# Second block's input tiles reordered, its norms and rotations moved between them, hidden chunks interleaved, one semaphore split

## What is computed

```python
x = first_block(...)      # dilated attention + pooling, gates, then 16384 experts of which 8 x 16 are used per token
# second block
h, hc = modulate(rmsnorm(x)), modulate(rmsnorm(ctx))            # 256 own and 256 context tokens
p = h @ w_in                                                    # 2048 -> q 1024, k 1024, v 1024, c_q 384, c_kv 256, k_rope 64
c_q, c_kv = rmsnorm(c_q) * q_norm_w, rmsnorm(c_kv) * kv_norm_w
q_mla, kv = c_q @ w_uq, c_kv @ w_ukv                            # 8 heads: 128 plain and 64 rotated columns of q, 128 k, 128 v
q_da, k_da, q_rope, k_rope = rope(...)                          # own tokens only
o = concat(diff_attention(q_da, k_da, v_da), attention(q_mla, k_mla, v_mla))
x = x + g1 * (o @ w_o)
g, u = split(modulate(rmsnorm(x)) @ w_up)                       # 2048 -> 2 x 5632
x = x + g2 * ((silu(conv3(g)) * u) @ w_down)                    # 5632 -> 2048
return rmsnorm(x)
```

## Time and profile before

| | |
|---|---|
| median of 3 runs | 3757.69 us (3756.13 to 3762.12) |
| the profiled execution: its own time | 3757.86 us |
| its span, first to last instruction | 3756.1 us |
| mean granted TensorE clock | 0.98 |
| input tiles of the second block, last matmul | 2684.0 us into the span |
| attention's first scores | 2773.4 us |
| stage "down", first matmul | 3481.3 us |

### The profile page before, as it was taken

How to read it: one execution, slowest core, us unless ns; L and a number is a source line. 1 busy time by engine, 2 the same in 40 slices (tenths; PEclk the granted TensorE clock), 3 DMA queues, 4 the chain that set the end, 5 groups by cost and what they waited for, 6 DMA issues and landing times.

```text
span 3756.1 us, 71853 instructions
## 1 busy us (share of the span) xinstructions
PE 3535.3 (94%) x27438; PEld 3378.2 (90%) x27438; DVE 2528.3 (67%) x4250; ACT 1734.2 (46%) x3141; POOL 116.6 (3%) x209
## 2 busy tenths in 40 slices
PE   1799999989999999999999999999988999999998
PEld 0799888988999999999999999889746899999998
DVE  7886432888757787878787888632266576766554
ACT  0542211454955454545454445632245565555443
POOL 0000000000200000000000000000000000000000
PEclk8899999999999999999999999999999999999999
DMA  9886775753666768676777777432210455555554
GB/s 411 340 331 254 280 275 221 265 181 135 222 250 225 300 239 314 238 300 249 285 265 288 263 289 269 171 105 97 82 53 23 157 191 191 196 194 183 175 179 146
DMA packets 118189, 829.33 MB, mean 221 GB/s; under 512 B 13105, under 2 KB 13233, under 8 KB 26801
## 3 DMA queue, kind: packets, MB, share of 16 engines
q1 hardware_dynamic: 88416, 619.20, 45.3%
q0 software_dynamic: 29520, 206.58, 14.4%
HBM read 806.86 MB, written 16.78 MB: 219 GB/s over the span
## 4 chain that ended last, share of the span: by engine, by line
PE 86%; DVE 5%; DMA 5%; ACT 3%; issue 1%; SPq 0%; POOL 0%; DVEq 0%; ACTq 0%
PE ps L1053 23%; PE ps L1054 23%; PE ps L1055 22%; PE ps L1028 9%; DMA arena<-in_ada 2%; ACT arena L549 2%; PE ps L1115 1%; PE ps L1117 1%; PE ps L1118 1%; DMA ring<-in_peer_down 1%; PE ps L1086 1%; DMA gates_scratch<-arena 1%; PE ps L1405 1%; PE ps L1042 0%; DVE ring_low L1552 0%
## 5 line engine op out<-in xcount | busy, mean ns | idle before, releaser
L549 ACT ACTIVATE w_parts<-ring 128x512 fp32r<-128x512 f32 x1288 | 801.3, 634 | 970.6 <-PE ps L1055 736.7
L1055 PE MATMUL ps<-x_high,ring_low 128*128 128x256 f32 (+1 forms) x4192 | 1182.8, 282 | 0.0
L1552 DVE TENSOR_TENSOR ring_low<-ring,w_parts 128x512 fp32r<-128x512 f32 x1288 | 836.6, 689 | 443.2 <-ACT w_parts L549 406.3
L1053 PE MATMUL ps<-x_high,w_parts 128*128 128x256 f32 (+1 forms) x2784 | 795.3, 286 | 82.2 <-DVE ring_low L1552 63.7
L1055 PEld LDWEIGHTS ps<-x_high,ring_low 128*128 128x128 f32 x4192 | 791.5, 189 | 7.8
L1054 PE MATMUL ps<-x_low,w_parts 128*128 128x256 f32 (+1 forms) x2784 | 792.9, 285 | 0.0
L1053 PEld LDWEIGHTS ps<-x_high,w_parts 128*128 128x128 f32 x2784 | 526.8, 189 | 91.8 <-DVE ring_low L1552 64.1
L1054 PEld LDWEIGHTS ps<-x_low,w_parts 128*128 128x128 f32 x2784 | 526.9, 189 | 8.2
L1552 DVE TENSOR_TENSOR ring_low<-ring,w_parts_ff 128x512 fp32r<-128x512 f32 (+1 forms) x544 | 357.7, 675 | 223.2 <-ACT w_parts_ff L549 217.3
L1053 PE MATMUL ps<-at_high,w_parts 128*128 128x256 f32 x1792 | 497.2, 277 | 0.0
L1055 PE MATMUL ps<-at_high,ring_low 128*128 128x256 f32 x1792 | 494.8, 276 | 0.0
(11 more groups left out here) (251 smaller groups left out, 5832.0 us busy)
## 6 DMA issues: line engine op xcount, KB each, us to landing
ada<-in_ada POOLq DMA_DIRECT2D x160, 1024.0 KB, 6.9
ring<-in_peer_down SPq DMA_DIRECT2D x128, 1024.0 KB, 4.9
ring<-in_peer_up SPq DMA_DIRECT2D x128, 1024.0 KB, 5.2
ring<-in_w_in SPq DMA_DIRECT2D x102, 1024.0 KB, 5.5
ring<-in_w_up SPq DMA_DIRECT2D x88, 1024.0 KB, 4.8
ring<-in_w_down SPq DMA_DIRECT2D x64, 704.0 KB, 4.0
arena<-in_ada SPq DMA_DIRECT2D x32, 1024.0 KB, 19.4
ring<-in_w_out SPq DMA_DIRECT2D x16, 1024.0 KB, 4.8
```

Of the source, the lines that this page charges most:

```text
L549: return nc.scalar.activation(*a, **k)
L1053: mm(to, w_high, high(k), start=(k == 0), stop=False)
L1055: ins = mm(to, w_low, high(k), start=False, stop=(k == k_all - 1))
L1552: vv.tensor_tensor(ring_low[:, slot, cols], ring[:, slot, cols], parts[:, m, 0:w].bitcast(F32), ALU.subtract).then_inc(lo_ready, 1)
```

## The change

- The order in the tables, in `w_in_2` and in every stream becomes q2, c2, k2, v2, then uq, then ukv. All loops over k2 and v2 on TensorE are written out. The columns of `w_uq` are put with the rotated part first.
- The norms of c_kv and c_q: ACT squares after k2's first output copy; TensorE sums after k2's third tile, c_q's into bank 5 (`b=5`); ACT takes the roots at tiles 18 and 19 of its loop, DVE the rest at 19 and 20. The squares and the rotations' temporaries lie in the free part of `cb`.
- The rotations of q2 and k2 (0 to 7): TensorE does two after each pair of v2 tiles; DVE does them at tiles 25, 27 and 29 of its loop and after the loop. Those of k_rope and the rotated part of q (8 to 12) lie between uq's tiles on TensorE.
- `hidden_high` and `hidden_low` become one buffer [44, 2, 256] at 32 KB: each chunk's low part directly behind its high part. `w_parts_ff` moves to 120 KB + 64 bytes.
- `G0`'s transfers count on a semaphore of their own, `g0_in`. DVE's `gate_held` waits for that alone; ACT waits for both.

```diff
-                  ("ahead", 16), ("first", 16), ("peer", 224), ("q2", 8), ("k2", 8), ("v2", 8), ("c2", 6), ("ukv", 16), ("uq", 16),
+                  ("ahead", 16), ("first", 16), ("peer", 224), ("q2", 8), ("c2", 6), ("k2", 8), ("v2", 8), ("uq", 16), ("ukv", 16),
...
-        HH, HL = split_room("hidden_high", 32, FF, T), split_room("hidden_low", 92 + 2 * APART, FF, T)
-        WF = split_room("w_parts_ff", 76 + APART, DEEP, PB * P)
+        hidden_both = split_room("hidden", 32, FF, 2, T)
+        HH, HL = hidden_both[:, :, 0, :], hidden_both[:, :, 1, :]
+        WF = split_room("w_parts_ff", 120 + APART, DEEP, PB * P)
...
                 pool_e.dma_start(G0[n // 8][:, n % 8, :], stage[n % 2][:, 0:16, :].rearrange("p c t -> p (c t)"))\
-                    .then_inc(g_stored[n % 2], 16)
+                    .then_inc(g0_in[n % 2], 16)
...
-                        act.wait_ge(g_stored[j], 32 * i)
+                        act.wait_ge(g0_in[j], 16 * i)
+                        act.wait_ge(g_stored[j], 16 * i)
...
                 if half:
                     for j in range(2):
-                        dve.wait_ge(g_stored[j], 32 * NBLK // 2)
+                        dve.wait_ge(g0_in[j], 16 * NBLK // 2)
...
@@ SP @@
+            for t in range(4):
+                load(TILES["uq"] + t, A["w_uq_2"][t], first + 30 + t, 12 * P)
             for t in range(2):
-                load(TILES["ukv"] + t, A["w_ukv_2"][t], first + 30 + t)
-            for t in range(4):
-                load(TILES["uq"] + t, A["w_uq_2"][t], OUTS["ukv"] if t < 2 else OUTS["ukv"] + 8 * (t - 1), 12 * P)
+                load(TILES["ukv"] + t, A["w_ukv_2"][t], OUTS["uq"] + 4 * (t + 1))
...
@@ ACT @@
+                if n == 18:
+                    root_of("kv", TA)
+                if n == 19:
+                    root_of("q", T)
...
+                if n == 15:
+                    act.wait_ge(acc_free, BANKS + OUTS["c2"] + 6)
+                    act_fn(sq_kv, ckv, ACT.Square).then_inc(squared, 1)
+                    act_fn(sq_q, cq, ACT.Square).then_inc(squared, 1)
-            act.wait_ge(acc_free, BANKS + OUTS["ukv"])
-            norm("kv", ckv, kn[:, 0:2, :], None, cols=TA)
-            norm("q", cq, sq2[:, 0:3, :], None)
...
@@ TensorE @@
+            for n in range(8):
+                o = OUTS["k2"] + n
+                bank(o)
+                split_tile("k2", 0, 0, n, ps[:, o % BANKS, :], W2, lambda k: X2H[:, k, :], lambda k: X2L[:, k, :],
+                           (14 + n) % RING)
+                if n == 2:
+                    norm_sum("kv", sq_kv, 2, TA)
+                    norm_sum("q", sq_q, 3, b=5)
+            def turn_rope(n):
+                if n >= 2:
+                    pe.wait_ge(roped, 12 + n - 1)
+                src, w = rope_step(n)
+                mm(ps[:, 4 + n % 2, 0:w], cst("perm2"), src, start=True, stop=True).then_inc(rotated, 1)
+            for m in range(4):
+                bank(OUTS["v2"] + 2 * m + 1)
+                split_values("v2", 0, 0, m,
+                             lambda tb: ps[:, (OUTS["v2"] + 2 * m + tb // 2) % BANKS, (tb % 2) * T:(tb % 2 + 1) * T],
+                             W2, X2H, X2L, 4, turn=22)
+                if m == 0:
+                    pe.wait_ge(acc_free, BANKS + OUTS["v2"])
+                    pe.wait_ge(var_ready, NORM_AT["q"] + 1)
+                turn_rope(2 * m)
+                turn_rope(2 * m + 1)
+            pe.wait_ge(scaled, before("q", "scaled") + 3)
+            for t in range(4):
...
+                if t == 1:
+                    turn_rope(8)
+                if t > 1:
+                    pe.wait_ge(acc_free, BANKS + OUTS["uq"] + 8)
+                    turn_rope(2 * t + 5)
+                    turn_rope(2 * t + 6)
             for t in range(2):
...
-            for n in range(13):
-                if n >= 2:
-                    pe.wait_ge(roped, 12 + n - 1)
...
@@ DVE @@
+                if n == 19:
+                    dve.wait_ge(final_ready, KC)
+                    norm("kv", ckv, ckv, vc("kv_norm_w_2"), cols=TA)
+                if n == 20:
+                    norm("q", cq, cq, vc("q_norm_w_2"), b=5)
+                if n in (25, 27, 29):
+                    turn_rope(n - 25)
+                    turn_rope(n - 24)
+            turn_rope(6)
+            turn_rope(7)
...
+            for n in range(8, 13):
+                turn_rope(n)
             dve.wait_ge(lam_exp, 1)
...
             dve.wait_ge(acc_free, BANKS + OUTS["wo2"])
-            for n in range(13):
-                src, w = rope_step(n)
```

More of the change, by code:

```diff
@@ L63 @@
 for _name, _n in (("qk", 24), ("v", 12), ("gate", 36), ("branch", 8), ("wo", 16), ("wq", 16),
-                  ("ahead", 16), ("first", 16), ("peer", 224), ("in2", 30), ("ukv", 2), ("uq", 4), ("wo2", 16), ("up", 88), ("down", 64)):
+                  ("ahead", 16), ("first", 16), ("peer", 224), ("in2", 30), ("uq", 4), ("ukv", 2), ("wo2", 16), ("up", 88), ("down", 64)):
     TILES[_name] = _t
@@ L396, in build_program @@
         g_stored = [sem(f"g_stored{j}") for j in range(2)]
+        g0_in = [sem(f"g0_in{j}") for j in range(2)]
         held_gated = sem("held_gated")
@@ L855, in out_copy, with root_of @@
                 return act_fn(to, src, ACT.Copy)
+            def root_of(name, cols):
+                act.wait_ge(var_ready, NORM_AT[name] + 1)
+                act_fn(rs[:, 0:cols], rs[:, 0:cols], ACT.Sqrt).then_inc(std_ready, 1)
             for n in range(31):
@@ L1016, in bank, with norm_sum @@
                 pe.wait_ge(acc_free, o + 1)
[L1018 removed]
+            def norm_sum(name, sqd, n, cols=T, b=4):
                 for k in range(n):
@@ L1056, in piece, with split_tile @@
                 return ins
-            def split_tile(name, i, per, u, to, parts, high, low):
+            def split_tile(name, i, per, u, to, parts, high, low, slot=None):
                 for j in range(PIECES):
@@ L1099, in split_summed, with split_values @@
                     sum_squares(run, c, c + 1, sq1, last=(c == KC - 1))
-            def split_values(name, i, per, m, bank_of, parts, high, low, tbs):
+            def split_values(name, i, per, m, bank_of, parts, high, low, tbs, turn=0):
                 for t in range(2):
@@ L1339, in _ @@
                 split_tile("c2", 0, 0, n, ps[:, o % BANKS, 0:TA - lo], W2, lambda k: X2H[:, k, lo:],
-                           lambda k: X2L[:, k, lo:])
-            norm_sum("kv", kn[:, 0:2, :], 2, TA)
-            pe.wait_ge(var_ready, NORM_AT["kv"] + 1)
-            norm_sum("q", sq2, 3)
-            pe.wait_ge(scaled, before("q", "scaled"))
+                           lambda k: X2L[:, k, lo:], n % RING)
+            for n in range(8):
[23 more added lines that the diff above has]
+            for t in range(4):
+                tile = TILES["uq"] + t
+                pe.wait_ge(w_slot[tile % RING], 16 * (tile // RING + 1))
+                for n in range(4):
+                    o = OUTS["uq"] + 4 * t + n
+                    bank(o)
+                    blocks(ps[:, o % BANKS, 0:T], tile, 3, lambda k: cq[:, k, :], at=3 * n).then_inc(acc_full, 1)
+                if t == 1:
[4 more added lines that the diff above has]
+                    turn_rope(2 * t + 6)
             for t in range(2):
@@ L1356, in _ @@
                     ins.then_inc(acc_full, 1)
-            pe.wait_ge(scaled, before("q", "scaled") + 3)
-            for t in range(4):
-                tile = TILES["uq"] + t
-                pe.wait_ge(w_slot[tile % RING], 16 * (tile // RING + 1))
-                for n in range(4):
-                    o = OUTS["uq"] + 4 * t + n
-                    bank(o)
-                    blocks(ps[:, o % BANKS, 0:T], tile, 3, lambda k: cq[:, k, :], at=3 * n).then_inc(acc_full, 1)
-            pe.wait_ge(acc_free, BANKS + OUTS["wo2"])
-            for n in range(13):
-                if n >= 2:
-                    pe.wait_ge(roped, 12 + n - 1)
-                src, w = rope_step(n)
-                mm(ps[:, 4 + n % 2, 0:w], cst("perm2"), src, start=True, stop=True).then_inc(rotated, 1)
+            pe.wait_ge(acc_free, BANKS + OUTS["wo2"])
             def s2(u):
```

71 lines of the change are left out of this document (32 added, 39 removed).

## The result

The changed kernel takes 3716.42 us (median of 4 runs, 3715.32 to 3722.56), the kernel before 3756.91 beside it (4 runs, 3753.40 to 3762.12): a ratio of 0.989, 95% interval 0.9879 to 0.9902. The prediction was 3713.3 us, range 3709.5 to 3731. The profiled executions took 3716.17 and 3757.86 us, with spans of 3714.4 and 3756.1: 41.7 us apart, where 44.5 were forecast.

What follows compares the result with a forecast made beforehand. TensorE, busy 94% of the span, was taken as the bound, so only its waits and matmul pace could gain: 26.4 + 2.3 + 15.8 = 44.5 us off 3757.86 gives 3713.3 us, range 3709.5 to 3731.

Steps and rivals of the forecast that it cites:

- Part 1: Second block's inputs to attention: moved norms and rotations leave TensorE no waits, 65.1 us for 91.5, 26.4 us gained.
- 8.17 us inside the input tiles: TensorE's matmuls for both norms' sums and rotations 0 to 5, still paid among the input tiles.
- 54.38 behind them: After the input tiles: rotations 6 to 12, uq and ukv's two tiles on TensorE without waits, 54.38 us.
- 2.52 for lambda: Tail before attention: ACT's last copy, table and exponential, and two tiny DVE operations, 2.52 us.
- Part 2: End of the gates: DVE starts earlier by waiting only for the 128 KB; 2.3 us gained, range 0 to 3.1.
- Part 3: Stage "down": hidden chunks side by side bring matmuls from 120.8 to 113.3 ns, 15.8 us gained.
- 885 matmuls in a window: Sign in "down": 885 matmuls in 100 us if right; 830 if wrong, putting the time near 3729.
- The rival that the layout does nothing: In "down", pieces or the sums' length cause the 120.8 ns; time 3729.1 us, chance 0.19.
- the worse layout: In "down", moving reads back and forth within 2 KB cost more; 3769.6 us at 140 ns per matmul, chance 0.03.
- both slow stages are those whose moving reads jump by an odd distance: Step for "down" and v2: odd distances between moving operands mark slow stages; "down" at 120.8 ns, v2 at 117.8.
- the weights' 64 bytes: In "down", weights stay offset by 64 bytes as in "up", so "up"'s 113.3 ns was taken.
- The start of attention gained no clock: Attention's first scores and next step: 0 us counted for a fuller clock, 1.4 us kept for the range.

Runs made afterwards that it cites:

- experiment 10: Changed kernel with the permutation matmul of rotations 0 to 5 made twice; 3722.88 us, ratio 0.9902 to the kernel before.
- experiment 1: Kernel before with only the gates' semaphore split, so DVE waits for G0's transfers alone; 3756.76 us, ratio 0.9996.
- experiment 12: Changed kernel with attention's first two scores issued between ukv's last outputs and ACT's first and lambda's exponentials taken earlier; 3712.30 us, ratio 0.9872 to the kernel before.
- experiment 3: Kernel before with only the hidden chunks' high and low parts put side by side; 3740.81 us, ratio 0.9952.
- experiment 5: Kernel before with `hidden_low` moved by 128 bytes, still 60 KB behind the high parts, at their offset modulo 256; 3742.10 us, ratio 0.9959.
- experiment 6: Kernel before with `hidden_low` 44 KB behind the high parts at the same offset, `w_parts_ff` at 120 KB + 64 bytes; 3741.77 us, ratio 0.9958.
- experiment 7: Kernel before with `hidden_low` 44 KB + 128 bytes behind the high parts and `w_parts_ff` at 120 KB + 192 bytes; 3771.42 us, ratio 1.003.
- experiment 8: Kernel before with `hidden_low` 44 KB + 128 bytes behind the high parts and `w_parts_ff` at 120 KB + 320 bytes; 3758.86 us, ratio 1.0002.
- experiment 9: Changed kernel with split weights at other offsets modulo 256: 128 for first inputs, up and down, 0 for output projection and second inputs; 3747.22 us, ratio 0.9976.
- experiment 4: Changed kernel with both input stages' split weights moved by 128 bytes, to the ring's offset 192; 3720.39 us, ratio 0.99 to the kernel before.

## Why the prediction was right

**Part 1: mechanism and terms right, 1.3 us too much.** Forecast were 8.17 us inside the input tiles, 54.38 behind them and 2.52 for lambda. Measured: the two norms' sums 3.01 and three pairs of rotations at 1.72, so 8.17; 54.34; and 2.63. That is 65.14 for 65.1, or 26.4 us gained. The traces show 25.1, since something else changed in the same stretch by 1.4: q2's first 96 matmuls took 13.88 us instead of 12.46. Both kernels come to the inputs after a stretch with little work for TensorE and begin them at half clock, and the changed one stayed there longer. The same 20 us, before and after:

```profile
2395.00:2415.00 20.00, 13.65 (x102) 13.52 (x103) 11.52 (x12) 18.01 (x28) 0.00 (x0) 0.83 0.05 14
```

```profile
2395.00:2415.00 20.00, 14.39 (x99) 14.34 (x100) 11.59 (x12) 18.73 (x30) 0.00 (x0) 0.74 0.02 3
```

In experiment 10, which has the changed kernel's order there too, the clock over these 20 us is 0.83, and in experiment 1, which has the old order, 0.75. So it belongs to the execution, not to the change, and the prediction had no term for it.

**Part 2: right at its place, mostly gone later.** 2.3 us forecast, 2.2 measured (4.24 to 2.05). But at the second block's inputs only 0.7 of a lead of 3.4 was left. In between lies "peer", the same code in both. TensorE waits five times there for a low part, 10.6 us in all before and 10.4 after, and behind some of these waits the clock is halved for a short while. Four such places in the changed kernel:

```profile
1310.00:1330.00 20.00, 17.95 (x144) 17.76 (x143) 13.56 (x24) 11.08 (x18) 0.53 (x1) 0.91 0.63 240
1490.00:1510.00 20.00, 17.94 (x144) 17.75 (x143) 13.48 (x24) 10.88 (x17) 0.53 (x1) 0.91 0.59 219
1665.00:1685.00 20.00, 17.86 (x143) 17.66 (x142) 12.89 (x23) 10.98 (x18) 0.53 (x1) 0.91 0.69 265
2020.00:2040.00 20.00, 18.06 (x145) 17.87 (x144) 13.28 (x23) 11.04 (x18) 0.53 (x1) 0.91 0.69 259
```

In the kernel before, only the third of these shows 0.91, and one more at 1840; the first of them, and that one:

```profile
1310.00:1330.00 20.00, 17.70 (x156) 17.51 (x155) 12.82 (x24) 11.05 (x18) 0.53 (x1) 1.00 0.79 305
1840.00:1860.00 20.00, 17.87 (x144) 17.68 (x143) 12.08 (x23) 9.63 (x17) 0.53 (x1) 0.91 0.72 291
```

Each costs 0.09 x 20 = 1.8 us, so two more cost some 3.5. The start of "first" gave 0.8 back, as its first 5.41 us had a clock of 0.68 for 0.53; that leaves the 2.7 lost. Over all fourteen traces of this document the clock fell behind two, three or four of these five waits. Experiments 1 and 12 have the same code there: the first kept 2.1 of its lead of 3.4 us, and the last began "first" 2.9 us behind the changed kernel and met it at the inputs, 0.1 behind. Which of the waits is followed by half clock changes from one execution to the next. A gain of 2 us in front of such a stage is real, but a single trace can't be relied on to show it at the end. That 1.2 us of the lead of 3.4 came from ahead of the gates was luck too.

**Part 3: the size right, the cause half right.** 15.8 us forecast, 15.9 measured, and 885 matmuls in a window as named. The rival that the layout does nothing (3729.1) fell with experiment 3, and the worse layout with it. The step that failed is the one that told slow stages from fast: "both slow stages are those whose moving reads jump by an odd distance". Distances of 1, 44 and 60 KB gave the same pace; it is the offset modulo 256 bytes, of the two moving operands and of the weights (experiments 5 to 9; 256 bytes further is the same place for the low parts in experiment 5 and for the weights in 8). The layout gained its 15.8 us because it put high and low at the same offset, which the reasoning didn't ask for: that part was luck. The prediction had also taken the weights' 64 bytes for a safe detail to keep "as in up". They were as important: at 192 they cost 4.4 ns per matmul in the 4224 of "up" (experiment 7), 18.6 us, more than the layout gives. And v2, cited as the second slow stage, didn't follow: with equal offsets it stayed slow. What in the chip makes the difference is open; the runs show the rule for this stream, not its cause.

The prediction weighed a rule of the Trainium skill (SBUF — State Buffer, Who interferes with whom), that PE never waits on anyone, which it took to mean that the layout is worth nothing. Experiments 3 and 5 differ from the kernel before in addresses alone, and their "down" is 15.9 us shorter, so a stream of matmuls isn't free of where its operands lie. The rule is about engines that wait for one another, which no run here tests, so it is the prediction's use of it that fell, and not the rule.

**Bounds.** The start of attention gained no clock (0 taken, 1.4 as the end of the range): "heads" starts 25.8 us ahead, as attention did. The written-out loops cost nothing visible: v2 kept its 117.8 ns. c2's narrow tiles ran at 113.4 ns in their new place. The sum's error of 2.8 us is thus 1.3 of clock at q2 and 1.5 between the gates and the inputs (2.7 lost, 1.2 won by luck before). Both are chance by what the other traces show.

## What to carry to other kernels

Where streams of matmuls of one shape run at different paces under a full clock with nothing waiting, compare the operands' addresses modulo 256 bytes early: count matmuls in equal windows, then move one buffer by 64 or 128 bytes. The map above is for 256 columns with a weight load for each; with 512 columns the order of two places was reversed (experiment 4), so it has to be made anew for another shape. And move only one, as buffers shared by two stages change both. Small norms and rotations belong between large tiles that are already fed, where TensorE pays only their matmuls; a last tail of small steps can be shortened further by starting the next stage between the last outputs.

## What the runs showed of the hardware that was not expected

- The pace of 256-column matmuls at full clock, with a weight load for each, depends on operand offsets modulo 256 bytes: 113.4, 116.7, 117.8, 119.2 or 120.9 ns, within 0.2 ns the same in every kernel with the same offsets (0.4 for the values at 192). The exception is the second tile of "heads", 113.3 ns in five traces and 118.9 in nine, from the same code. Between the best and the worst lie 16 us in a stage of 2112 matmuls.
- It isn't a matter of distance, and equal offsets of the moving operands aren't enough: with activations at 0, weights at 64 are faster than at 0, 128 and 192. With the low parts at 128, the order of 64 and 192 is reversed.
- The Trainium skill (TensorE: Matmul & The Clock Gate, Wait — 56ns, not 53.3ns?) gives some 2.5 ns above the columns' own time as the floor from one matmul to the next, an estimate of 109.2 ns for 256 columns. No stream here came to that; the best, with a weight load for each, was 113.3.
- After a wait of about 2.2 us in "peer" the granted clock falls for a moment, or doesn't, in the same code: behind two of five such waits in one execution and four of five in the other, at 1.8 us each.
